# Values turned by VectorE and rewritten through memory instead of transposed on TensorE, and four steps of the last phase put in another order

## The chip, the cores and the metric

One core of one Trainium2 chip runs the kernel. The metric is the device time of one execution in microseconds (us); the median of the runs is compared. Engines in the profile: PE is TensorE's matmul, PEld its weight load, DVE is VectorE, ACT is ScalarE, POOL is GpSimd, SP is SyncE (here it issues all transfers).

## The reference: what is computed

A decoder layer on 1024 tokens of width 1024, in float32. Three groups of attention heads (head size 64) read one input projection of the normalised rows; a memory group of 4 heads reads 256 memory tokens.

```
h = rmsnorm(x, norm_w);  proj = h @ w_in
sb_q, sb_k, sb_v, fx_q, fx_k, fx_v, f_logit, m_q, gate = split(proj)
sb_out = stick_breaking_attention(sb_q, sb_k, sb_v)      # 8 heads
fx_out = forgetting_attention(fx_q, fx_k, fx_v, cumsum(log_sigmoid(f_logit + b)))   # 8 heads
m_out  = memory_attention(m_q, rmsnorm(mem) @ w_mem_kv)  # 4 heads
y = per_head_rmsnorm(concat(sb_out, fx_out, m_out)) * out_norm_w * silu(gate)
out = rmsnorm(x + y @ w_out, final_norm_w)
```

## The kernel before

**Stages.** After a start of about 60 us (rows squared, scaled and turned into `hT`, memory keys and values), the kernel runs ten phases, numbered 0 to 9: two of the memory heads, then `fx` and `sb` in turn, four pairs of heads each (phases 2, 4, 6, 8 are forgetting attention, 3, 5, 7, 9 stick-breaking). A phase is 16 ticks, one for each block of 128 queries of a head and half; the first and third group of four ticks have the long rows (640 to 1024 keys), the others the short ones (128 to 512). Ticks are counted through: phase 9 (`LAST`) begins at tick 144 (`X0`), and eight more ticks follow tick 159.

**A tick.** Every engine has its own list, written out tick by tick, and the order in it is fixed. TensorE does the scores of the tick (`scores`, L1023 and L1024), some steps of the projection (`project`, L867 to L869; in the last phase the output projection, L912), then the value products of the tick before (`values`, L1056 and L1057), the transposes of finished probability rows (`transposes`, L1037), the small transposes (`small`) and more projection. ScalarE makes the upper part of each transposed tile (`upper_part`, L1266), VectorE the lower one (`lower_part`, L1876), both needed by the value products of the next tick. Each float32 matrix is used as an upper and a lower part whose sum is the value.

**The values.** The projection leaves a head pair's values as 128 channels by 512 tokens in a bank, twice for a phase (`c` 0 and 1). VectorE copies them to `v_raw` (L1710; in `negL` or in a row of `work`). TensorE transposes the four blocks of 128 (`small`, piece "VT", L984) into `SMALL_BANK`, ScalarE copies the upper part to the heads' region (`values_hi`, L1223), VectorE subtracts for the lower one (`finish_small`, L1774). This stands in phase p-1 for phase p, for p from 2 to 9. The memory values ("MT") go the same way, and totals ("NT") too. Other pieces of the list `SMALL` don't touch TensorE: N1 (squares of the outputs summed per head) and N3 (the outputs' scale and the gate).

**Weights.** Tiles of 512 KB come through one buffer `w_raw`: `load_tile` (L606, L610) waits until ScalarE (L1165) and GpSimd (L1534) have split the tile before. SyncE does its list in order: behind `load_tile` stand the copies of the keys (L615, L616), `load_negL` (L625), the store of the scales (L649) and their spread fetch (L667).

**The last phase.** From tick 142 on SyncE fetches the split output weights (`fetch_w_out`, L713, 20 transfers of 512 KB), then blocks of the finished outputs (`load_y`, L722), split by ScalarE (`y_hi`, L1358) and VectorE (`y_lo`, L1890), and rows of x (`load_x`, L735) that are added to the partial outputs (L1730) and stored (L739). The gate of the last phase lies in `w_raw`, which is also a place for rows of x: it is stored in `silu_dram` (L814), and `load_x(1)` waits for that. At the end the last phase's own outputs are added: `end_outputs` (L1077), four calls with n from 0 to 3 and two later; call n from 2 on waits for the sum n-2 (`end_sum`, L1950), which for n below 4 waits for the partial rows (`load_part`, L744). The first call waits for the last scales (N3 at tick 165: L1811, L1816, then `y_end_hi` L1383 and `y_end_lo` L1895).

## Time and profile before

| | |
|---|---|
| median of 3 runs | 793.46 us (793.13 to 793.98) |
| profiled execution, its own time | 793.03 us |
| its span, first to last instruction | 791.1 us, so 1.9 us lie around it |
| PE busy | 776.6 us, 98% |
| DVE, ACT, POOL busy | 605.0, 445.7, 257.7 us (76%, 56%, 33%) |
| granted TensorE clock, mean | 0.998 of full speed |
| DMA queue of SyncE | 37648 packets, 92.50 MB, 36.1% of 16 engines |

The busy time of PE is that of matmuls that overlap in the pipeline, and their ends are modelled; a start and the next start tell more. Starts of one line in the timeline are the engine's own.

### The profile page before, as it was taken

The numbers are of one execution on the slowest core, as the hardware profiler recorded it, in microseconds if no ns is written. First come the engines' busy times: TensorE is split into PE (matmuls) and PEld (weight loads), VectorE is DVE, ScalarE is ACT, GpSimd is POOL, SyncE is SP. The second block draws the span as 40 slices with busy tenths as digits, with TensorE's granted clock in tenths as the row PEclk, the third lists the DMA queues.
The fourth block names the chain that finished last, engine by engine and source line by source line (L and its number), as shares of the span: only waits on it lengthen the run. The fifth ranks groups of instructions, "written<-read, shape, count | busy, mean of one in ns | idle before, by whom it ended". The sixth has DMA issues, their size and how long they took to land.

```text
span 791.1 us, 11916 instructions
## 1 busy us (share of the span) xinstructions
PE 776.6 (98%) x4030; PEld 653.2 (83%) x4030; DVE 605.0 (76%) x1206; ACT 445.7 (56%) x920; POOL 257.7 (33%) x440
## 2 busy tenths in 40 slices
PE   8999999999999999999999999999999999999997
PEld 8878887888888888888888888888888887878775
DVE  6877687776789777768977777898767688685676
ACT  7767765556646555665745667465555574542232
POOL 1112733242156326223823521383234124210000
PEclk9999999999999999999999999999999999999999
DMA  9413824124113412521261142106213398233523
GB/s 355 134 63 141 278 98 148 54 69 106 67 54 98 144 40 69 134 67 54 65 175 41 68 125 77 54 27 178 76 55 81 110 386 300 82 107 107 187 96 143
DMA packets 37708, 93.25 MB, mean 118 GB/s; under 512 B 5000, under 2 KB 13192, under 8 KB 36624
## 3 DMA queue, kind: packets, MB, share of 16 engines
q1 hardware_dynamic: 37648, 92.50, 36.1%
q8 instruction: 32, 0.52, 0.3%
q14 instruction: 28, 0.23, 0.1%
HBM read 61.91 MB, written 21.66 MB: 106 GB/s over the span
## 4 chain that ended last, share of the span: by engine, by line
PE 85%; DVE 7%; DMA 2%; ACT 2%; issue 2%; SPq 0%; POOL 0%; ACTq 0%; DVEq 0%; POOLq 0%
PE banks L867 16%; PE banks L869 15%; PE banks L868 15%; PE banks L1037 8%; PE banks L912 8%; PE banks L1057 5%; PE banks L1024 4%; PE banks L1056 4%; PE banks L1023 4%; PE banks L1108 1%; DMA hT<-wo_dram 1%; PE banks L984 1%; DMA work<-part_dram 1%; PE banks L1077 1%; DVE pT L1876 1%
## 5 line engine op out<-in xcount | busy, mean ns | idle before, releaser
L867 PE MATMUL banks<-hT,w_parts 128*128 128x512 f32 x576 | 237.6, 412 | 0.3 <-DVE sb_heads L1735 0.2
L869 PE MATMUL banks<-hT,w_parts 128*128 128x512 f32 x576 | 225.8, 392 | 0.0
L868 PE MATMUL banks<-hT,w_parts 128*128 128x512 f32 x576 | 225.4, 391 | 0.0
L1266 ACT ACTIVATE pT<-banks 128x512 fp32r<-128x512 f32 x208 | 92.4, 497 | 126.7 <-PE banks L1037 126.4
L1876 DVE TENSOR_TENSOR pT<-banks,pT 128x512 fp32r<-128x512 f32 x208 | 108.4, 563 | 66.6 <-ACT pT L1266 65.3
L869 PEld LDWEIGHTS banks<-hT,w_parts 128*128 128x128 f32 x576 | 108.1, 188 | 24.5
L867 PEld LDWEIGHTS banks<-hT,w_parts 128*128 128x128 f32 x576 | 108.5, 188 | 15.8 <-DVE sb_heads L1735 1.0
L868 PEld LDWEIGHTS banks<-hT,w_parts 128*128 128x128 f32 x576 | 109.0, 189 | 13.6
L1534 POOL TENSOR_TENSOR w_parts<-w_raw,w_parts 128x1024 fp32r<-128x1024 f32 x34 | 81.4, 2395 | 91.9 <-ACT w_parts L1165 91.9
L1541 POOL TENSOR_SCALAR_AFFINE_SELECT work<-work 128x128 f32<-128x128 f32 x64 | 30.4, 475 | 192.7 <-ACT work L1243 192.7
L1836 DVE TENSOR_TENSOR_SCAN work<-work 128x639 f32<-128x639 f32 (+3 forms) x64 | 90.7, 1418 | 0.7 <-POOL work L1541 0.6
L1242 ACT ACTIVATE work<-banks 128x512 f32<-128x512 f32 (+2 forms) x96 | 47.4, 494 | 71.5 <-PE banks L1024 60.3
L1037 PE MATMUL banks<-ident,work 128*128 128x128 f32 x640 | 87.1, 273 | 0.0
L1037 PEld LDWEIGHTS banks<-ident,work 128*128 128x128 f32 x640 | 74.8, 140 | 10.0
L912 PE MATMUL banks<-hT,fx_heads 128*128 128x512 f32 x288 | 73.6, 395 | 1.3 <-DMA hT<-wo_dram 1.3
L912 PEld LDWEIGHTS banks<-hT,fx_heads 128*128 128x128 f32 x288 | 52.7, 188 | 11.9 <-DMA hT<-wo_dram 1.7
L1259 ACT ACTIVATE work<-work,npeak 128x640 f32<-128x640 f32 (+3 forms) x64 | 49.7, 777 | 18.9 <-DVE npeak L1865 18.8
L1842 DVE TENSOR_TENSOR work<-work 128x639 f32<-128x639 f32 (+3 forms) x64 | 52.0, 813 | 6.6
L1856 DVE CUSTOM_DVE_ANT_0 work<-banks,negL 128x512 f32<-128x512 f32 (+3 forms) x56 | 32.1, 574 | 21.7 <-PE banks L1024 20.5
L1243 ACT ACTIVATE work<-banks 128x512 f32<-128x512 f32 (+2 forms) x96 | 47.7, 497 | 0.0
L1552 POOL TENSOR_SCALAR_AFFINE_SELECT diag<-negL 128x128 f32<-128x128 f32 x64 | 21.1, 333 | 73.1 <-DVE npeak L1865 73.0
L1023 PE MATMUL banks<-sb_heads 128*128 128x256 f32 (+2 forms) x128 | 41.5, 324 | 1.1 <-issue 1.0
(258 smaller groups left out, 1355.9 us busy)
## 6 DMA issues: line engine op xcount, KB each, us to landing
w_raw<-in_w_tiles SPq DMA_DIRECT2D x36, 512.0 KB, 3.9
hT<-wo_dram SPq DMA_DIRECT2D x14, 512.0 KB, 8.4
fx_heads<-fx_heads SPq DMA_DIRECT2D x8, 512.0 KB, 7.8
negL<-negL_dram SPq DMA_DIRECT2D x8, 512.0 KB, 6.1
yT_dram<-silu SPq DMA_DIRECT2D x8, 512.0 KB, 4.1
sb_heads<-sb_heads SPq DMA_DIRECT2D x8, 512.0 KB, 6.7
negL<-yT_dram SPq DMA_DIRECT2D x8, 512.0 KB, 4.9
work<-in_x SPq DMA_DIRECT2D x6, 512.0 KB, 6.7
```

Source lines behind the costliest of these rows:

```text
L867: pe.matmul(o, w[0][:, k, :], hT[:, 0, k, tok], start=(k == 0), stop=False)
L868: pe.matmul(o, w[0][:, k, :], hT[:, 1, k, tok], start=False, stop=False)
L869: mm = pe.matmul(o, w[1][:, k, :], hT[:, 0, k, tok], start=False, stop=(k == KT - 1))
L912: mm = pe.matmul(banks[:, bank_of(q + c - p.c), :], yt, wo_part(j, r)[:, c, :], start=(fresh and j == order[0] and (l, r) == (0, 0)), stop ...
L1023: pe.matmul(o, q, k[:, 0, c0:c1], start=True, stop=False)
L1037: mm = pe.transpose(banks[:, T_BANK + n % 2, j * P:(j + 1) * P], p_row(u + j)[:, t.s * P:(t.s + 1) * P], ident[:, :])
L1259: act.activation(p_row(u), p_row(u), ACT.Exp, bias=top, accum_out=total).then_inc(fx_p, 1)
L1266: act.activation(pT[:, n % 3, 0, cols], banks[:, T_BANK + n % 2, cols], ACT.Copy).then_inc(t_hi, 1)
L1534: pool.tensor_tensor(w_part(n, 1), by_tiles(w_raw_of(n)), w_part(n, 0).bitcast(F32), ALU.subtract).then_inc(w_lo, 1)
L1836: dve.tensor_tensor_scan(left, left, left, 1.0, ALU.mult, ALU.bypass).then_inc(scanned, 1)
L1842: dve.tensor_tensor(b[:, 0:w - 1], b[:, 0:w - 1], f[:, 1:w], ALU.mult).then_inc(sb_p, 1)
L1876: dve.tensor_tensor(pT[:, n % 3, 1, cols], banks[:, T_BANK + n % 2, cols], pT[:, n % 3, 0, cols].bitcast(F32), ALU.subtract).then_inc(t_lo, 1)
```

## The change

The values are no longer transposed by TensorE. VectorE writes `v_raw` with a transpose of 32x32 blocks, SyncE stores it in a buffer in memory with four transfers per piece that put the blocks at their transposed places (runs of 32 numbers, 128 bytes), and fetches it in rows of 512 bytes to the place of the lower part. ScalarE copies it to the upper part, VectorE subtracts in place. Two waits that told when `v_raw` was free now ask for the store. Ticks: the fetch is at tick 7 of the phase (or later), the two splits at ticks 13 and 15 of it (for phase 9 at ticks 141 and 143; for phase 3 at 45 and 47; for phase 2 at 21 and 25). The plan of the projection steps stays as it is. In the last phase the store of the gate moves behind the fetches of the output weights, `y_hi` and `y_lo` move behind `upper_part` and `lower_part` (and behind the tick's small pieces), and the last N3 moves ahead of `output`.

```diff
-READY_BEFORE = firsts(1 if p.what in ("VT", "MT", "NT") else 0 for p in SMALL)
+def values_ticks():
+    out = []
+    for of in range(2, N_PH):
+        for c in range(2):
+            done = READ_TICK[piece_of("V", c, of)] - 1
+            fetch = max(done + 2, UNITS * (of - 1) + 7) if of > 2 else done + 8
+            out.append((of, c, fetch, max(fetch + 3, UNITS * (of - 1) + 13 + 2 * c) if of > 2 else fetch + 3))
+    return out
@@ sync
+                if p.what == "V":
+                    store_values(q)
                 if closes_tile(p) and p.what == "K":
                     copy_keys(p.of, q)
+            def store_values(q):
+                p = PIECE[q]
+                sp.wait_ge(piece_done, q + 1)
+                rows = v_dram[p.of, p.c, :, :].rearrange("(j k) (i d) -> i k j d", k=Q4, d=Q4)
+                for i in range(P // Q4):
+                    sp.dma_start(rows[i], v_raw(p.of, p.c)[i * Q4:(i + 1) * Q4, :].rearrange("k (j d) -> k j d", d=Q4)).then_inc(v_out[p.c], 16)
+            def fetch_values(of, c):
+                sp.wait_ge(v_out[c], 64 * (of - 1))
+                if of > 2:
+                    sp.wait_ge(pv_done, STEP0[4 * (of - 1)])
+                else:
+                    for j in (1, 2):
+                        sp.wait_ge(wo_out[j], 32)
+                sp.dma_start(v_in_rows(of, c).bitcast(F32).rearrange("p b x c -> p b (x c)"),
+                             v_dram[of, c, :, :].rearrange("(b p) w -> p b w", p=P)).then_inc(v_in[c], 16)
+                if c == 1 and PHASES[of][0] == "fx":
+                    load_negL(PHASES[of][1], 1)
-                if p.what == "VT" and p.c == 1 and PHASES[p.of][0] == "fx":
-                    sp.wait_ge(small_done, n + 1)
-                    load_negL(PHASES[p.of][1], 1)
@@ sync, last phase
-            sp.wait_ge(piece_done, piece_of("G", 1, LAST) + 1)
-            sp.dma_start(silu_dram[:, :], gate_of(LAST)).then_inc(silu_out, 16)
             sp.wait_ge(piece_ready, piece_of("G", 1, LAST - 1) + 1)
             for j in range(6, NB):
                 fetch_w_out(j)
             for j in range(NB, NT_OUT):
                 fetch_w_out(j)
+            sp.wait_ge(piece_done, piece_of("G", 1, LAST) + 1)
+            sp.dma_start(silu_dram[:, :], gate_of(LAST)).then_inc(silu_out, 16)
             load_x(1)
@@ tensor
-                if p.what == "VT":
-                    pe.wait_ge(piece_done, piece_of("V", p.c, p.of) + 1)
-                    for b in range(4):
-                        mm = pe.transpose(o[:, b * P:(b + 1) * P], v_raw(p.of, p.c)[:, b * P:(b + 1) * P], ident[:, :])
-                    pe.wait_ge(small_done, small_of("VT", 1, x0.ph) + 1)
+                    pe.wait_ge(v_done, 2 * (x0.ph - 1))
@@ scalar
+            def values_hi(of, c):
+                act.wait_ge(v_in[c], 16 * (of - 1))
+                act.activation(v_of(region_of(of))[:, 4 * c:4 * c + 4, 0::3, :], v_in_rows(of, c).bitcast(F32), ACT.Copy).then_inc(v_hi, 1)
-                    act.wait_ge(small_ready, READY_BEFORE[small_of("VT", 1, t.ph)] + 1)
+                    for c in range(2):
+                        act.wait_ge(v_out[c], 64 * (t.ph - 1))
-                for n in Y_AT[i]:
-                    y_hi(n)
                 if 1 <= i <= N_UNITS and UNIT[i - 1].kind != "sb" and not softmax_ends:
...
+                for of, c, _, at in VALUES:
+                    if i == at:
+                        values_hi(of, c)
+                for n in Y_AT[i]:
+                    y_hi(n)
@@ vector
-                    dve.tensor_copy(v_raw(p.of, p.c), src).then_inc(piece_done, 1)
+                    dve.transpose(v_raw(p.of, p.c), src).then_inc(piece_done, 1)
+            def values_lo(of, c):
+                dve.wait_ge(v_hi, 2 * (of - 2) + c + 1)
+                v = v_of(region_of(of))[:, 4 * c:4 * c + 4, :, :]
+                dve.tensor_tensor(v[:, :, 1:3, :], v[:, :, 1:3, :].bitcast(F32), v[:, :, 0::3, :].bitcast(F32), ALU.subtract).then_inc(v_done, 1)
-                for n in Y_AT[i]:
-                    y_lo(n)
+                ended = [n for n in SMALL_AT[i] if (SMALL[n].what, SMALL[n].of) == ("N3", LAST)]
+                for n in ended:
+                    finish_small(n)
                 if i in OUT_AT:
                     output(OUT_AT[i])
...
                 for n in T_AT[i]:
                     lower_part(n)
+                for of, c, _, at in VALUES:
+                    if i == at:
+                        values_lo(of, c)
...
+                for n in Y_AT[i]:
+                    y_lo(n)
```

## Rows read from the trace of the kernel before

**Rows 1.** The page: the engines' busy time over the span.
```profile
PE 776.6 (98%) x4030; PEld 653.2 (83%) x4030; DVE 605.0 (76%) x1206; ACT 445.7 (56%) x920; POOL 257.7 (33%) x440
```
**Rows 2.** The largest wait of PE from 60 us on: total us, times, longest.
```profile
PE banks L1056 <- DVE pT L1876: 1.4, 2, 1.1
```
**Rows 3.** Timeline of PE around one value transposition: start us, length us.
```profile
118.19 0.39 PE L869 MATMUL banks<-hT,w_parts 128*128 128x512 f32 x1
118.42 0.60 PE L984 MATMUL banks<-ident,negL 128*128 128x128 f32 x4
118.78 0.48 PE L867 MATMUL banks<-hT,w_parts 128*128 128x512 f32 x1
119.09 0.40 PE L868 MATMUL banks<-hT,w_parts 128*128 128x512 f32 x1
```
**Rows 4.** Groups by line, whole span: count, busy us, mean ns, idle before.
```profile
L984 PE MATMUL banks<-ident,negL 128*128 128x128 f32 x32 | 4.8, 273 | 0.0
L1710 DVE COPY work<-banks 128x512 f32<-128x512 f32 x8 | 5.5, 684 | 0.0
L1790 DVE STREAM_TRANSPOSE o_tmp<-banks 128x512 f32<-128x512 f32 x20 | 14.1, 705 | 1.7 <-ACT banks L1287 1.7
L1383 ACT ACTIVATE sb_heads<-silu 128x512 fp32r<-128x512 f32 x2 | 1.3, 632 | 3.2 <-DVE silu L1816 3.2
```
**Rows 5.** The largest wait of ACT, 129 to 640 us: total us, times, longest.
```profile
ACT pT L1266 <- PE banks L1037: 102.7, 61, 3.8
```
**Rows 6.** Transfers: packets and the scales' store alone (314 to 317.5 us), then a median.
```profile
q1 hardware_dynamic: 144, 0.02, 3.1%
...
r_dram<-r_rows SPq DMA_DIRECT2D x1, 16.0 KB, 1.4
...
negL<-yT_dram SPq DMA_DIRECT2D x8, 512.0 KB, 4.9
```
**Rows 7.** Timeline of SyncE in phase 3: issues of two weight tiles, start us.
```profile
238.65 0.33 SPq L610 DMA_DIRECT2D w_raw<-in_w_tiles  x1
250.81 0.33 SPq L610 DMA_DIRECT2D w_raw<-in_w_tiles  x1
```
**Rows 8.** Timeline at the start of the last phase, ACT and then PE.
```profile
635.60 0.48 ACT L1243 ACTIVATE work<-banks 128x384 f32<-128x384 f32 x1
636.14 0.51 PE L1023 MATMUL banks<-sb_heads 128*128 128x512 f32 x1
```
**Rows 9.** Last phase: two stalls of PE; one window (its last two numbers: DMA share, GB/s).
```profile
658.99 0.98 PE L912 MATMUL banks<-hT,fx_heads 128*128 128x512 f32 x3 [1.31 <-DMA hT<-wo_dram]
704.22 0.47 PE L1056 MATMUL banks<-pT,sb_heads 128*128 128x512 f32 x1 [1.11 <-DVE pT L1876]
...
652.30:653.60 1.30, 1.30 (x7) 1.08 (x6) 1.20 (x2) 0.00 (x0) 0.00 (x0) 1.00 1.04 403
```
**Rows 10.** Timeline of DVE and ACT, ticks 157 and 163 to 165.
```profile
701.41 1.23 DVE L1890 TENSOR_TENSOR fx_heads<-negL,fx_heads 128x1024 fp32r<-128x1024 f32 x1 [0.87 <-ACT fx_heads L1358]
733.46 0.63 ACT L1297 ACTIVATE work<-head 128x512 f32<-128x512 f32 x1 [4.75 <-DVE head L1683]
736.94 0.71 DVE L1811 STREAM_TRANSPOSE banks<-work 128x512 f32<-128x512 f32 x1
738.47 0.63 ACT L1383 ACTIVATE sb_heads<-silu 128x512 fp32r<-128x512 f32 x1 [2.96 <-DVE silu L1816]
```
**Rows 11.** The chain that ended last, its steps from 734 to 752 us.
```profile
733.99 1.05 ACT fx_heads L1358
735.07 1.24 DVE fx_heads L1890
736.32 0.37 SPq L722
...
743.37 1.24 DVE work L1950
...
752.19 3.02 PE banks L1077 x12
```

More of the change, by code:

```diff
@@ L290, in small_pieces @@
             out.append(Small("N3", c, ph - 1, UNITS * ph + N3_AT + N3_LATER.get(ph - 1, 0)))
-    taken = [p.tick for p in out]
-    for q, p in enumerate(PIECE):
-        if p.what == "V":
-            tick = max(READ_TICK[q] + 1, UNITS * (p.of - 1) + (9 + 2 * p.c if p.of == 2 else 6))
-            while tick in taken:
-                tick += 1
-            taken.append(tick)
-            out.append(Small("VT", p.c, p.of, tick))
     for c in (1, 0):
@@ L307 @@
 SMALL_AT = [[n for n, p in enumerate(SMALL) if p.tick == i] for i in range(N_TICKS)]
-READY_BEFORE = firsts(1 if p.what in ("VT", "MT", "NT") else 0 for p in SMALL)
+READY_BEFORE = firsts(1 if p.what in ("MT", "NT") else 0 for p in SMALL)
 NT_BEFORE = firsts(1 if p.what == "NT" else 0 for p in SMALL)
-VT_BEFORE = firsts(1 if p.what in ("VT", "MT") else 0 for p in SMALL)
+MT_BEFORE = firsts(1 if p.what == "MT" else 0 for p in SMALL)
+def values_ticks():
[6 more added lines that the diff above has]
+    return out
+VALUES = values_ticks()
 def next_phase(i, at, later={}):
@@ L444, in v_raw, with v_in_rows @@
             return place[:, c * CW:(c + 1) * CW]
+        def v_in_rows(of, c):
+            return v_of(region_of(of))[:, 4 * c:4 * c + 4, 1:3, :]
         def gate_of(ph):
@@ L794, in _ @@
                     piece_end(q)
+                for of, c, fetch, _ in VALUES:
+                    if i == fetch:
+                        fetch_values(of, c)
                 for n in SMALL_AT[i]:
@@ L977, in small @@
                 p = SMALL[n]
-                if n and p.what in ("VT", "MT", "NT"):
+                if n and p.what in ("MT", "NT"):
                     pe.wait_ge(small_done, n)
                 o = banks[:, SMALL_BANK, :]
-                if p.what == "VT":
-                    pe.wait_ge(piece_done, piece_of("V", p.c, p.of) + 1)
-                    for b in range(4):
-                        mm = pe.transpose(o[:, b * P:(b + 1) * P], v_raw(p.of, p.c)[:, b * P:(b + 1) * P], ident[:, :])
-                elif p.what == "MT":
+                if p.what == "MT":
                     pe.wait_ge(piece_done, piece_of("memV", p.c, None) + 1)
@@ L1207, in split_next, with mem_values_hi @@
                     split_hi(w_follows(PIECE[q].tile))
-            def values_hi(n):
+            def mem_values_hi(n):
                 p = SMALL[n]
                 act.wait_ge(small_ready, READY_BEFORE[n] + 1)
-                if p.what == "MT":
-                    for b in range(MB):
-                        ins = act.activation(mem_v[:, b, p.c, 0::3, :],
-                                             banks[:, SMALL_BANK, b * P:(b + 1) * P].rearrange("p (h c) -> p h c", h=2), ACT.Copy)
-                    ins.then_inc(vt_hi, 1)
-                    return
-                if p.of > 2:
-                    act.wait_ge(pv_done, STEP0[4 * (p.of - 1)])
-                elif p.c == 0:
-                    for j in (1, 2):
-                        act.wait_ge(wo_out[j], 32)
-                act.activation(v_of(region_of(p.of))[:, 4 * p.c:4 * p.c + 4, 0::3, :],
-                               banks[:, SMALL_BANK, :].rearrange("p (b h c) -> p b h c", b=4, h=2), ACT.Copy).then_inc(vt_hi, 1)
+                for b in range(MB):
+                    ins = act.activation(mem_v[:, b, p.c, 0::3, :],
+                                         banks[:, SMALL_BANK, b * P:(b + 1) * P].rearrange("p (h c) -> p h c", h=2), ACT.Copy)
+                ins.then_inc(mt_hi, 1)
+            def values_hi(of, c):
+                act.wait_ge(v_in[c], 16 * (of - 1))
+                act.activation(v_of(region_of(of))[:, 4 * c:4 * c + 4, 0::3, :], v_in_rows(of, c).bitcast(F32), ACT.Copy).then_inc(v_hi, 1)
             def sigmoids(u):
@@ L1442, in _ @@
             for n in range(len(MEM_VALUES_AT)):
-                values_hi(n)
+                mem_values_hi(n)
             evacuate(7)
@@ L1490, in _ @@
                 for n in SMALL_AT[i]:
-                    if SMALL[n].what in ("VT", "MT"):
-                        values_hi(n)
+                    if SMALL[n].what == "MT":
+                        mem_values_hi(n)
                     if SMALL[n].what == "N1" and SMALL[n].of == LAST:
@@ L2082, in _ @@
                     lower_part(n)
+                for of, c, _, at in VALUES:
+                    if i == at:
+                        values_lo(of, c)
                 for n in SMALL_AT[i]:
-                    if n not in early:
+                    if n not in early + ended:
                         finish_small(n)
```

11 lines of the change are left out of this document (4 added, 7 removed).

## The prediction

> **What bounds the kernel now.** I read the page first: PE is busy 98% of the span, DVE 76%, ACT 56% [rows 1]. A busy PE can hide stalls here, since matmuls overlap in the pipeline and their ends are modelled, so I read PE's waits next. From 60 us on the largest of them is 1.4 us in all [rows 2]; the reader is to see that over 700 us nothing else keeps PE waiting for longer. The counter-view is the waits of ACT: in 500 us of the middle it waited 102.7 us for PE's transposes, 61 times, 1.7 us each on average [rows 5]. The engines behind PE wait for it, not it for them. So PE's own instructions set the pace, and one that disappears from PE's list is worth its distance from start to start. In the last phase it is different: there PE has two stalls of over 1 us [rows 9], and the chain that ended last leaves PE for ACT, DVE, SyncE and a transfer [rows 11].
>
> **Term 1: the transposes on PE.** Phases 2 to 9 have two pieces of values each, so 16 groups of four transposes go, 64 instructions, in two groups of 32 of which one is shown [rows 4]. What is one group worth? From the start of the matmul ahead (118.19) to the start of the second behind (119.09) it is 0.90 us [rows 3]. Without the four, two starts of 512 columns would lie there, 0.23 us each by the first pair of the same rows (118.19 to 118.42), 0.46 in all. That leaves 0.44 us. In most ticks other transposes (L1037) stand just ahead, and a first matmul behind transposes is longer by some 0.08 us (118.78 to 119.09 is 0.31), which may stay; so 0.36 to 0.44 is the bound from both sides, 5.8 to 7.0 us for 16. I take 7.0, since the 0.36 is only the distance to the first matmul and what stays is paid by the groups ahead anyway. The mean of 273 ns per transpose [rows 4] would give 17.5 us; it holds the modelled drain and I don't take it. The Trainium skill, page "Perfetto Trace Analysis", section "Identifying the Most-Contended Engine", says that TensorE's matmul busy time is a bad measure, because matmuls are pipelined; by busy durations the sum would be 10.5 us better than by starts. The trace sides with that rule: the row of four says 0.60 us of length, while the next matmul starts after 0.36.
>
> **Term 2: what VectorE and ScalarE do instead.** The copy of 684 ns becomes a 32x32 transpose of the same shape, 705 ns in the row nearest to it, 16 times 0.02 us. The upper part is now read from SBUF, 632 ns in the nearest row [rows 4]; the subtraction keeps its size. Under the cover of PE all this costs nothing. It moves: for the phases with long rows the splits leave ticks 7 and 8 (two of the dense ones) for ticks 13 and 15, whose rows are short. Cover gone, it would be 32 pieces of 0.65 us, 21 us, but only where ACT has less than the 1.7 us it waits on average. One place has no cover: the upper part for phase 9 at tick 143. Behind it on ScalarE stand the y block, the exponentials, a table load and the first sigmoids of phase 9, and PE's second scores wait for a bank that these read: the read started at 635.60, lasted 0.48, and PE started at 636.14 [rows 8]. That is 0.06 us behind it, so no slack. One ACT step more, 0.63 less the overlap of neighbours, is **+0.5 us** on PE (bounds 0 and 0.63). I take it for this phase alone, since for the others no y block stands between.
>
> **Term 3: the transfers.** Each piece is stored by four transfers of 512 packets of 128 bytes, 2048 in all, and fetched in 512 packets of 512 bytes. 16 such stores are 32768 packets, nearly as many as the kernel has. No row shows such a store, so I bound it. Below: the scales' store, 128 packets of 128 bytes, landed in 1.4 us, and 144 packets took 3.1% of 16 engines in 3.5 us, 12 ns of an engine each [rows 6]. With that, 2048 packets over 16 engines add 1.5 us, some 3 us to landing. Above: if the whole 1.4 us were per packet, 16 times 1.4 are 22 us. The nearest row in count is the fetch of y, 1024 packets of 512 bytes in 4.9 us; twice that is 10 us. I take 3 to 7 us. Who waits for it? SyncE itself, which asks for the store ahead of the fetch. In phase 3 the store follows the weight tile of 238.65, and the next thing that SyncE does late is the tile of 250.81, for which it waits anyhow [rows 7]. Between them lie 12 us, so a store of 7 us and a fetch of 4 us are hidden, and the splits come only at ticks 13 and 15. `load_negL`, which stood in the crowd behind 250.81, now goes out ahead of it; a small relief, no gain on PE. I take **0**.
>
> **Term 4: the gate's store behind the weights.** PE waits at 658.99 for the fetched output weights; to the idle 1.31 us come 0.16 that the modelled end hides (0.39 of length against 0.23 between starts, rows 3), 1.47 in all. The DMA engines are full there; the gate's 512 KB take 1.3 us of them (403 GB/s, share 1.04) [rows 9]. Taken out of the queue ahead, every later weight lands 1.3 us earlier, and PE comes 0.5 later by term 2: the stall goes, **-1.5 us** (bounds -1.0 and -1.5). What is late next: `load_x(1)` and the y block 2 behind it go out only once it has landed behind all of these weights. ScalarE may wait for the block, but it does so behind the upper parts of its tick, and PE needs the block two ticks on.
>
> **Term 5: blocks behind transposed parts.** At 704.22 PE waits for the lower part of tick 157: 1.11 idle, 1.27 with the hidden 0.16 [rows 9]. Ahead of that part DVE did the y block, 1.23 us, and sat idle 0.87 for it [rows 10]. Both move behind it, 2.1 us against a stall of 1.27: it goes, **-1.3 us**.
>
> **Term 6: the same move at the end, and the last scales first.** Here the rule turns. The chain that ended last runs: y block 6 on ACT (733.99) and DVE (735.07, done 736.31), the issue of y block 7 by SyncE (736.32), behind it final norm weights and the partial rows, the first sum on DVE (743.37), the last head sums, the second sum, and PE's fourth end call at 752.19 [rows 11]. In the new order tick 165 has the scales first. They can start when the spread is there, 733.46 + 0.63 = 734.09. From the start of their turn to the end of ScalarE's copy it was 736.94 to 739.10, 2.16 us [rows 10], so 736.25 now. Only then does ScalarE begin y block 6, 1.05 us, and DVE its lower part, 1.24: done at 738.5 instead of 736.3. All that SyncE issues behind it, y block 7 and the partial rows, is late by 2.2 us, and so are both sums and PE's fourth call: **+2.2 us**. What the scales first bring, the end of PE's wait of 0.84 idle us ahead of its first call, doesn't count, since the fourth call waits anyhow. Bounds: +2.2 where the chain holds, and -1.0 where the partial rows have slack that I don't see.
>
> **Sum.** -7.0 + 0.5 + 0 - 1.5 - 1.3 + 2.2 = -7.1 us. Against the profiled execution's own time, 793.03, that is 785.9; the median of the runs is 0.4 higher, so **786.4 us**. Its own range, with the bounds of the terms, is 785.9 to 788.2 (1.2 more by term 1, 0.1 by term 2, 0.5 by term 4; 0.5 less by term 2).
>
> **Rivals.**
> - *The end doesn't give it back* (12%): the sums are early enough, and the scales' wait goes. Then 3.2 us less, 783.2. For it: nothing in the rows, except that 7 us pass from the issue at 736.32 to the sum at 743.37, in a crowd of transfers that could thin out. Against it: the first three steps of rows 11 follow each other within 0.03 us.
> - *ACT and DVE take over* (12%): the value transposes stood between a step's transposes and its products and gave ACT and DVE 0.4 us more to make the parts. Where that was the last slack, PE now waits. For it: DVE is at 76% [rows 1], and that is a mean over phases of which some must be denser. Against it: 1.7 us of average wait. If half the groups pay, the first term is -3.5: 789.9.
> - *Small packets hold SyncE, and it ends slower* (4%): store and fetch together over 12 us delay the next weight tile and the keys' copies in phases 3, 5 and 7. At the upper bound of 22 us and a fetch of 4, SyncE is 14 us late in each; if all of it reaches PE, 42 in all, 828. It is slower than before from 2.4 us of lateness a phase, a store of about 10.4 us. The Trainium skill, page "VectorE: DVE Perf Modes", section "The three transpose paths", warns that a plain DMA copy that transposes by strides is 19 times slower than the hardware's own way. The 12 ns per packet of 128 bytes speak against it here.
> - *Nothing comes of it* (4%): what PE saves is lost at a phase's start where Q and keys are waited for: 793.
>
> **Numbers.** Forecast 68%. The range that leaves out less than 2 in 10 reaches from the first rival to the second: 783.2 to 789.9. A measurement of this kernel tells 0.2%, 1.6 us, from nothing. Faster: forecast and the first two rivals, 92%; same 4%; slower 4%.
>
> **What would show it.** L984 gone, and PE's starts 0.23 apart where it stood; the small-packet count up by 32768, with each of the four store transfers landing in 3 to 7 us; no wait of PE for wo_dram and none at tick 158; the start of phase 9 with about 0.5 us more of a wait for ACT; and y block 7 issued 2 us later counted from the last transposes, with the fourth end call waiting some 3 to 4 us for a sum. It would be wrong if L1266 or L1876 now release PE in the middle, if a store of values takes above 10 us to land, or if the partial rows come early.

## The result, and the profile after

The changed kernel takes **805.05 us** (median of 4 runs, 803.12 to 805.27) beside 793.72 (793.13 to 795.39) for the kernel before on the same chip: ratio 1.0137, interval 1.0125 to 1.015. It is slower by 11.3 us where 7.1 us of gain were forecast, and lies outside the range of the prediction. The profiled execution took 803.12 us, the fastest of the four, and its span is 801.4 (before: 791.1).

The page of the changed kernel, its engines and packets, and then the mean granted clock of the core (before: 0.998):

```profile
PE 775.8 (97%) x3966; PEld 650.3 (81%) x3966; DVE 611.2 (76%) x1206; ACT 446.5 (56%) x920; POOL 260.9 (33%) x440
...
PEclk9999998999999999999999999999999999999999
...
DMA packets 79949, 101.65 MB, mean 127 GB/s; under 512 B 39048, under 2 KB 55432, under 8 KB 78864
```
```profile
core 0: 801.4 us, clock 0.990
```

PE has 64 instructions less than in [rows 1], as meant, and is busy for 0.8 us less in a span that is 10.3 us longer. The packets under 512 bytes went from 5000 to 39048. One slice of the clock fell from 9 to 8: the seventh, 120 to 140 us.

The waits of the changed kernel (total us, times, longest):

```profile
PE banks L1053 <- ACT work L1282: 8.9, 2, 6.5
PE banks L1107 <- DVE work L1979: 4.5, 1, 4.5
...
ACT fx_heads L1249 <- DMA fx_heads<-v_dram: 9.8, 2, 7.2
```

Before, the largest wait of PE from 60 us on was 1.4 us [rows 2]. Now PE waits 8.9 us, in two pieces, for an exponential of ScalarE, and the last row says for what ScalarE waits: the upper part of the values (L1249) that a transfer brings back from DRAM. The other new wait, 4.5 us, is the fourth end call of PE.

Where along the kernel the time goes shows best when the start of the same unit of work is read in both traces, a unit's first scores matmul. The table is worked out so, start after minus start before; the last entry is the difference of the spans:

```
tick    22    24     28     30     36     48     64     66     70     74
us   +0.25 +4.00 +11.82 +12.39 +12.01 +11.15 +10.78 +11.47 +11.47 +10.61
tick    96     98    102    106   119   122   134   138   144   145   149   150   158   159   end
us   +9.93 +10.51 +10.51  +9.65 +9.68 +8.81 +8.96 +8.10 +8.10 +8.62 +8.63 +7.48 +7.48 +6.05 +10.3
```

So 12.1 us are lost between ticks 22 and 30, the second half of phase 1, in which the values for phase 2 are made ready. Then the curve falls by 0.41 to 0.45 wherever four transposes are gone, as term 1 had it, rises by 0.69 where phase 4 starts, by 0.58 where phase 6 does and by 0.52 at phase 9 (tick 145), falls by 1.1 at the gate's store (tick 150) and by 1.4 at tick 159, and rises by 4.25 at the end. (Rises of 0.3 and less in between, 0.9 us together, I did not follow.)

**The values for phase 2.** ScalarE of the changed kernel, timeline, at the two upper parts for phase 2 (start us, length us, in brackets the idle time ahead of it and what ended it), and PE where it waits for them:

```profile
109.99 0.63 ACT L1249 ACTIVATE fx_heads<-fx_heads 128x512 fp32r<-128x512 f32 x1 [2.64 <-DMA fx_heads<-v_dram]
...
127.09 0.63 ACT L1249 ACTIVATE fx_heads<-fx_heads 128x512 fp32r<-128x512 f32 x1 [7.20 <-DMA fx_heads<-v_dram]
127.63 0.46 ACT L1282 ACTIVATE work<-banks,npeak 128x256 f32<-128x256 f32 x1
```
```profile
111.65 0.38 PE L1053 MATMUL banks<-sb_heads 128*128 128x256 f32 x1 [2.46 <-ACT work L1282]
...
128.23 0.58 PE L1053 MATMUL banks<-sb_heads 128*128 128x256 f32 x1 [6.48 <-ACT work L1282]
...
129.25 0.63 PE L902 MATMUL banks<-hT,w_parts 128*128 128x512 f32 x1
129.68 0.63 PE L903 MATMUL banks<-hT,w_parts 128*128 128x512 f32 x1
130.10 0.63 PE L901 MATMUL banks<-hT,w_parts 128*128 128x512 f32 x1
...
132.89 0.39 PE L901 MATMUL banks<-hT,w_parts 128*128 128x512 f32 x1
133.12 0.40 PE L902 MATMUL banks<-hT,w_parts 128*128 128x512 f32 x1
```

The exponential that PE waits for at 128.23 (L1282, 127.63) isn't late by itself; it stands behind the upper part on ScalarE, which is blocked for 7.20 us by a fetch. And the wait is not the whole loss. Behind it PE's matmuls of 512 columns start 0.43 us apart (129.25, 129.68, 130.10) and not 0.23 as at the end of the fence: that is the lower of the clock's two levels, 1.2 GHz. Summed over the two places, the starts are 12.9 us further apart than in undisturbed rows: 8.94 of it are the two idle times, 0.3 what the modelled ends hide of them, and 3.6 matmuls at or near the lower clock. The two groups of transposes that are gone here give 0.9 back.

Why does the fetch come so late? SyncE of the changed kernel, timeline, and the instruction of GpSimd that its weight tile waits for:

```profile
104.22 1.13 SPq L665 DMA_DIRECT2D fx_heads<-v_dram  x1
122.90 0.34 SPq L621 DMA_DIRECT2D w_raw<-in_w_tiles  x1
123.34 0.37 SPq L665 DMA_DIRECT2D fx_heads<-v_dram  x1
```
```profile
120.45 2.38 POOL L1563 TENSOR_TENSOR w_parts<-w_raw,w_parts 128x1024 fp32r<-128x1024 f32 x1
```

The second fetch (123.34) could have gone out much earlier (fetch_early, below, issues it at 104), but SyncE stood from 105.35 to 122.90 at the weight tile ahead of it in its list, which needs the room that GpSimd's split frees at 122.83. The fetch landed at 127.07 and took only 3.7 us. In the kernel before, the same tile was issued at 119.47 and PE did not wait in that stretch. This chain is that of the second piece. The first piece's fetch did not stand behind the tile: it was issued at 104.22 and took 5.7 us to land, in a stretch in which the DMA engines were busy with the split output weights, a tile and the next piece's stores (95 to 112 us: the queue's packets take 83.9% of 16 engines). By the table above (ticks 22 to 30) the first piece cost some 4 us and the second some 8.

**The transfers.** The page of the changed kernel, its DMA issues (KB each, median us from issue to landing):

```profile
v_dram<-negL SPq DMA_DIRECT2D x32, 64.0 KB, 3.2
...
fx_heads<-v_dram SPq DMA_DIRECT2D x8, 256.0 KB, 3.1
v_dram<-work SPq DMA_DIRECT2D x32, 64.0 KB, 2.6
```

A store of 512 packets of 128 bytes lands in 2.6 to 3.2 us in the median, the 64 of them in 1.7 to 5.6. Term 3 had taken 3 to 7.

**The end.** The chain that ended last, of the changed kernel (start us, us), with the steps that answer to [rows 11], and a timeline of GpSimd and DVE there:

```profile
742.27 1.06 ACT fx_heads L1384
743.35 2.04 DVE fx_heads L1919
745.41 0.37 SPq L753
...
746.50 5.87 DMA work<-part_dram
...
752.47 1.24 DVE work L1979
...
760.00 1.23 DVE work L1979
761.27 4.32 PE banks L1107 x12
```
```profile
742.57 1.73 POOL L1594 TENSOR_TENSOR silu<-silu,yT 128x512 f32<-128x512 f32 x1 [14.07 <-DVE yT L1914]
...
743.35 2.03 DVE L1919 TENSOR_TENSOR fx_heads<-negL,fx_heads 128x1024 fp32r<-128x1024 f32 x1 [0.20 <-ACT fx_heads L1384]
```

From the issue of y block 7 to the first sum it takes 7.06 us (before 7.05), from there to the second 7.53 (before 7.56): the chain moved as a whole. Its head moved by 9.09 us (736.32 to 745.41), PE by 6.05, so the end is late by 3.04. Of these 2.2 are the ones of term 6; the other 0.8 is the lower part of block 6, which took 2.03 us and not 1.23 as in [rows 10]. Then come the twelve matmuls, 4.32 us in place of 3.02, the first six of them again at the lower clock.

### The profile page after: what moved, and what is told of

Same layout as the page of the kernel before. It is cut to its first block, busy times and chain, and to the rows that moved or that the text cites. A ratio compares the mean times of both kernels' runs of the same rounds, so it can differ in the third digit from the quotient of the medians.

```text
span 801.4 us, 11859 instructions
## 1 busy us (share of the span) xinstructions
PE 775.8 (97%) x3966; PEld 650.3 (81%) x3966; DVE 611.2 (76%) x1206; ACT 446.5 (56%) x920; POOL 260.9 (33%) x440
## 4 chain that ended last, share of the span: by engine, by line
PE 83%; DVE 6%; DMA 3%; ACT 3%; issue 2%; POOL 1%; SPq 1%; ACTq 0%; DVEq 0%; POOLq 0%
PE banks L901 15%; PE banks L903 15%; PE banks L902 15%; PE banks L946 9%; PE banks L1067 8%; PE banks L1053 4%; PE banks L1087 4%; PE banks L1054 4%; PE banks L1086 4%; DMA fx_heads<-v_dram 1%; PE banks L1138 1%; PE banks L1107 1%; DMA hT<-wo_dram 1%; DMA work<-part_dram 1%; POOL w_parts L1563 1%
## 5 line engine op out<-in xcount | busy, mean ns | idle before, releaser
L1292 ACT ACTIVATE pT<-banks 128x512 fp32r<-128x512 f32 x208 | 92.4, 497 | 124.5 <-PE banks L1067 124.2
L1905 DVE TENSOR_TENSOR pT<-banks,pT 128x512 fp32r<-128x512 f32 x208 | 108.3, 562 | 59.0 <-ACT pT L1292 57.8
L1570 POOL TENSOR_SCALAR_AFFINE_SELECT work<-work 128x128 f32<-128x128 f32 x64 | 32.6, 509 | 184.8 <-ACT work L1269 184.8
L1067 PEld LDWEIGHTS banks<-ident,work 128*128 128x128 f32 x640 | 74.8, 140 | 10.1
```

The source lines that it names most:

```text
L1067: mm = pe.transpose(banks[:, T_BANK + n % 2, j * P:(j + 1) * P], p_row(u + j)[:, t.s * P:(t.s + 1) * P], ident[:, :])
L1292: act.activation(pT[:, n % 3, 0, cols], banks[:, T_BANK + n % 2, cols], ACT.Copy).then_inc(t_hi, 1)
L1905: dve.tensor_tensor(pT[:, n % 3, 1, cols], banks[:, T_BANK + n % 2, cols], pT[:, n % 3, 0, cols].bitcast(F32), ALU.subtract).then_inc(t_lo, 1)
```

## The experiments

Each median stands beside that of the kernel before, measured on the same chip in the same session: 793.51 us for vals_only, order_only, split_late and big_packets; 793.97 for y6_early, scales_late, splits_13_14 and best_a; 793.87 for fetch_early, rows_first, gate_early and best_b. Line numbers shift by at most 2 between the versions of the changed kernel; order_only has those of the kernel before.

### vals_only: the values' path alone
The changed kernel with the whole last phase in the order of before (the gate's store, the y blocks, the last scales).
```
             fetch_w_out(0)
+            sp.wait_ge(piece_done, piece_of("G", 1, LAST) + 1)
+            sp.dma_start(silu_dram[:, :], gate_of(LAST)).then_inc(silu_out, 16)
...
                     sigmoids(i)
+                for n in Y_AT[i]:
+                    y_hi(n)
...
                     turn_scales(ph)
-                ended = [n for n in SMALL_AT[i] if (SMALL[n].what, SMALL[n].of) == ("N3", LAST)]
-                for n in ended:
-                    finish_small(n)
+                for n in Y_AT[i]:
+                    y_lo(n)
```


> The values' new path alone, the last phase in its old order. Theory A (the values for phase 2 are fetched too late, ScalarE waits for them in ticks 21 and 25 and PE behind it; it costs 12 us; the end of the last phase costs about 2 us more): 802.3 us, stalls of PE of 2.5 and 6.5 us near 112 and 128 us, and the sum at the end on time, with no wait of PE above 1.1 us there. Theory B (the 32768 small packets slow all engines' accesses and transfers everywhere): also about 802 to 805, but spread over phases 2 to 8.

Measured: 801.3 us (799.63 to 802.29), ratio 1.0098 [1.008, 1.0115], span 798.7. PE has both waits for phase 2's values, 2.39 and 6.34 us, and not the one of 4.5 at the end. The values' path alone loses 7.8 of the 11.3 us; what the last phase loses shows in the next run.

### order_only: the last phase alone
The kernel before with the four steps in the last phase and its values left as they were: the edit of vals_only the other way round, made to the kernel before.
```
             fetch_w_out(0)
-            sp.wait_ge(piece_done, piece_of("G", 1, LAST) + 1)
-            sp.dma_start(silu_dram[:, :], gate_of(LAST)).then_inc(silu_out, 16)
...
                     turn_scales(ph)
-                for n in Y_AT[i]:
-                    y_lo(n)
+                ended = [n for n in SMALL_AT[i] if (SMALL[n].what, SMALL[n].of) == ("N3", LAST)]
+                for n in ended:
+                    finish_small(n)
```

> The kernel before with the four steps of the last phase reordered, no new path for the values. Theory A: the stalls at 659 and 704 us go (-2.7), the partial rows land later and PE's fourth end call waits 4.5 us and then runs at the lower clock for a while (+4.3): 795.3, slower than before by 1.6. Rival (the reorder is a gain, the loss at the end comes from the values' transfers): 791.0, no long wait at the end.

Measured: 796.14 us (794.93 to 797.56), ratio 1.0034 [1.0023, 1.0045], span 793.4. Unit by unit against the kernel before, it is 1.1 us earlier behind the gate's store and another 1.4 at tick 159, as terms 4 and 5 had it, and then loses 4.6. PE, timeline, the fourth end call:

```profile
753.00 2.44 PE L1077 MATMUL banks<-w_parts,fx_heads 128*128 128x512 f32 x6 [4.51 <-DVE work L1950]
755.23 2.38 PE L1077 MATMUL banks<-hT,sb_heads 128*128 128x512 f32 x6
```

Six matmuls take 2.23 us from start to start of the two rows, where 1.49 are the rule (in y6_early the same two starts are 746.13 and 747.62). The last phase's steps by themselves lose 2.6 us; with the values' 7.8 that is 10.4 of the 11.3.

### split_late: phase 2's splits 8 and 6 ticks later
```
-            out.append((of, c, fetch, max(fetch + 3, UNITS * (of - 1) + 13 + 2 * c) if of > 2 else fetch + 3))
+            out.append((of, c, fetch, max(fetch + 3, UNITS * (of - 1) + 13 + 2 * c)))
```
For phase 2 the splits now stand at ticks 29 and 31 and not at 21 and 25. The fetches stay where they are, behind the weight tile.

> The changed kernel, but the two splits of phase 2's values stand at ticks 29 and 31 instead of 21 and 25; the fetches and all packets stay. Theory A: both stalls near 112 and 128 us go and the clock stays up: 805.05 - 12.3 = 792.7. Theory B (packets): at most 2 us better, 803.

Measured: 791.97 us (791.04 to 793.87), ratio 0.9982 [0.9972, 0.9991]. ScalarE, timeline, the same two upper parts:

```profile
124.17 0.63 ACT L1249 ACTIVATE fx_heads<-fx_heads 128x512 fp32r<-128x512 f32 x1
128.91 0.61 ACT L1249 ACTIVATE fx_heads<-fx_heads 128x512 fp32r<-128x512 f32 x1
```

No idle time ahead of either, and no wait of PE for L1282 above 0.02 us. One condition taken out turns 1.4% slower into 0.2% faster. The same stores and fetches are all there; what cost the time was asking for their result too early. The new ticks have a smaller price of their own. VectorE's subtraction of the second piece now falls beside GpSimd's split of a tile (129.09, 2.37 us), and PE waits behind it where phase 2 starts, DVE and then PE:

```profile
129.56 2.45 DVE L1846 TENSOR_TENSOR fx_heads<-fx_heads 128x512 fp32r<-128x512 f32 x1 [0.21 <-ACT fx_heads L1249]
...
134.16 0.50 PE L1053 MATMUL banks<-fx_heads 128*128 128x512 f32 x1 [0.77 <-DVE peak L1885]
```

### big_packets: the same bytes in few packets
```
-                for i in range(P // Q4):
-                    sp.dma_start(rows[i], v_raw(p.of, p.c)[i * Q4:(i + 1) * Q4, :].rearrange("k (j d) -> k j d", d=Q4)).then_inc(v_out[p.c], 16)
+                sp.dma_start(v_dram[p.of, p.c, :, :].rearrange("(p r) w -> p (r w)", p=P), v_raw(p.of, p.c)).then_inc(v_out[p.c], 16)
```
One store of 128 rows of 2 KB in place of four of 512 packets each. The edit leaves out the blocks' move to their transposed places, so this kernel computes with mixed-up values and serves for its time alone. It changes two things at once: the packets' size, and what SyncE has to issue, one store for a piece and not four.

> The changed kernel, but each piece of values is stored in one transfer of 128 rows of 2 KB instead of four transfers of 512 packets of 128 bytes; the blocks' new places are left out of the computation, so the values are mixed up. Ticks, waits and all else stay. Theory A: the second and larger stall (6.6 us) stays, since SyncE stands behind a weight tile's wait and not behind packets; the first (2.6 us) may shrink, as SyncE issues faster in phase 1: 801 to 805. Theory B: 793 or less.

Measured: 801.97 us (800.52 to 803.1), ratio 1.0105 [1.009, 1.012], span 801.3 (the changed kernel: 801.4). Packets and ScalarE of this run:

```profile
DMA packets 48461, 101.65 MB, mean 127 GB/s; under 512 B 5512, under 2 KB 21896, under 8 KB 47376
```
```profile
107.75 0.63 ACT L1247 ACTIVATE fx_heads<-fx_heads 128x512 fp32r<-128x512 f32 x1 [0.57 <-DMA fx_heads<-v_dram]
124.83 0.63 ACT L1247 ACTIVATE fx_heads<-fx_heads 128x512 fp32r<-128x512 f32 x1 [7.84 <-DMA fx_heads<-v_dram]
```

The small packets are gone, and the wait for the second fetch is 7.84 us, longer than in the changed kernel. The first fetch's wait does fall, from 2.64 to 0.57: it is issued at 100.48 and not at 104.22. So 2.3 us of this loss (10.1 us at tick 30 and not 12.4) hang on the four stores, by their packets or by their issues, which this run doesn't tell apart; the large wait doesn't. That the two spans are equal is chance: behind its fourth end call this execution gives 2.1 us back, where its twelve matmuls take 5.29 us and not 4.17 because the lower clock lasts longer. Each beside its own kernel before, the medians stand 2.9 us apart.

### fetch_early: the second fetch ahead of the weight tile
```
-            fetch = max(done + 2, UNITS * (of - 1) + 7) if of > 2 else done + 8
-            out.append((of, c, fetch, max(fetch + 3, UNITS * (of - 1) + 13 + 2 * c) if of > 2 else fetch + 3))
+            fetch = max(done + 2, UNITS * (of - 1) + 7) if of > 2 else done + (8 if c == 0 else 7)
+            out.append((of, c, fetch, max(fetch + 3, UNITS * (of - 1) + 13 + 2 * c) if of > 2 else done + 11))
```
The splits of phase 2 stay at 21 and 25; only the fetch of the second piece goes out one tick earlier in SyncE's list, which is ahead of the tile.

> The changed kernel with one thing moved: the fetch of phase 2's second piece stands at tick 21 of SyncE's list, ahead of the weight tile of tick 22, not behind it. Splits stay at ticks 21 and 25. Theory A (the 6.6 us stall is SyncE's wait for GpSimd's split of the tile ahead, not the landing): that stall goes with the lower clock behind it, 7.7 us; the first stall of 2.6 stays: 805.05 - 7.7 = 797.3. Rival (the landing itself is slow in that stretch): 803 or more.

Measured: 798.3 us (797.77 to 798.38), ratio 1.0053 [1.0038, 1.0068]. SyncE issues both fetches together, and ScalarE doesn't wait for the second:

```profile
103.59 1.79 SPq L665 DMA_DIRECT2D fx_heads<-v_dram  x2
...
123.73 0.34 SPq L621 DMA_DIRECT2D w_raw<-in_w_tiles  x1
```
```profile
110.81 0.63 ACT L1249 ACTIVATE fx_heads<-fx_heads 128x512 fp32r<-128x512 f32 x1 [3.34 <-DMA fx_heads<-v_dram]
...
120.48 0.63 ACT L1249 ACTIVATE fx_heads<-fx_heads 128x512 fp32r<-128x512 f32 x1
```

The splits stand where they stood, the packets are the same, and the 7.2 us are gone: it was the order in SyncE's list. What stays is the first fetch, 3.34 us on ScalarE and 3.15 on PE, and six matmuls of 512 columns at the lower clock behind it. And PE waits 1.30 us at 125.36 for an exponential. The rows show its cause, the subtraction of the second piece on VectorE, which takes 2.83 us in place of 0.69 beside GpSimd's split of a tile and holds the row maxima (L1899) behind it:

```profile
121.35 2.83 DVE L1846 TENSOR_TENSOR fx_heads<-fx_heads 128x512 fp32r<-128x512 f32 x1
...
121.25 2.39 POOL L1563 TENSOR_TENSOR w_parts<-w_raw,w_parts 128x1024 fp32r<-128x1024 f32 x1
```

### y6_early: the block of tick 165 back in its old place
split_late, and for tick 165 alone the y block stands ahead of the parts again.
```
+                for n in Y_AT[i] if i == END_N3_TICK else []:
+                    y_hi(n)
...
+                for n in Y_AT[i] if i == END_N3_TICK else []:
+                    y_lo(n)
```


> split_late, with the one y block of tick 165 (block 6) ahead of the scales and the output again, on ScalarE and VectorE; the other six blocks stay behind the transposed parts. Theory A (the late partial rows hold the second sum, PE's fourth end call waits 4.7 us and runs at the lower clock for some 2.5 us after it): both losses go, 791.97 - 6.3 = 785.7. Rival (the wait comes from the store of the gate behind the weights, which shifts the rows of x and with them the partial rows): no change, 792.

Measured: 787.1 us (786.69 to 787.49), ratio 0.991 [0.9895, 0.9924], mean clock 1.0. The fourth end call waits 1.01 us, not 4.51, and its matmuls run at the higher clock. Some 5 us come from one y block's place (4.9 between the medians, 5.3 with each beside its own kernel before).

### rows_first: only SyncE's order at the end
split_late, and y block 7 goes out behind the final norm's weights and the partial rows.
```
             for n in range(6):
-                load_y(n + 2)
+                if n < 5:
+                    load_y(n + 2)
...
                 load_part(n)
+            load_y(7)
```


> split_late, with y block 7's load on SyncE behind the final norm weights and the four partial rows instead of ahead of them. Orders of ScalarE and VectorE stay as changed, so y block 6 is as late as in the change. Theory A (PE's 4.7 us wait at the end runs over SyncE's list: block 6, then the load of block 7, which waits for it, then the partial rows): the wait and the lower clock go, 791.97 - 6 = 786. Rival (the wait comes over ScalarE's and VectorE's own later work): 791 to 792.

Measured: 786.0 us (785.75 to 786.67), ratio 0.9901 [0.9886, 0.9916]. SyncE and PE, timelines:

```profile
719.63 2.76 SPq L775 DMA_DIRECT2D work<-part_dram  x3
733.62 0.37 SPq L753 DMA_DIRECT2D negL<-yT_dram  x1
```
```profile
744.97 1.67 PE L1109 MATMUL banks<-w_parts,fx_heads 128*128 128x512 f32 x6
```

Block 6 is as late here as in split_late (its lower part takes 2.03 us in both), but the partial rows don't stand behind it, and PE has no idle time of note at the fourth call. The head of the chain in [rows 11] was late only through SyncE's list.

### scales_late: without the last scales first
split_late with the last scales turned where they were.
```
-                ended = [n for n in SMALL_AT[i] if (SMALL[n].what, SMALL[n].of) == ("N3", LAST)]
-                for n in ended:
-                    finish_small(n)
...
-                    if n not in early + ended:
+                    if n not in early:
```

> split_late, with the last scales behind the output again; the y blocks stay late. Theory A: the y block's place does it, the scales' own move is a small gain: the block ends another 0.7 us later, so 792.7. Rival (the scales ahead of everything at tick 165 are what holds the block): the wait shrinks by 2 us or more, 789.

Measured: 792.57 us (791.8 to 793.63), ratio 0.9984 [0.9974, 0.9993]; the wait of 4.51 us at the fourth call is there. The scales' place is worth 0.6 us at most: the delay comes from the block's place, not from theirs. On ScalarE the block still stands behind the copy of the scales here (L1409 at 730.85, block 6 at 731.38); it starts later than in split_late, and its lower part takes 1.22 us and not 2.03.

### gate_early: the gate's store ahead of the weights again
y6_early with the store of `silu_dram` in front of the fetches of the output weights.
```
             fetch_w_out(0)
+            sp.wait_ge(piece_done, piece_of("G", 1, LAST) + 1)
+            sp.dma_start(silu_dram[:, :], gate_of(LAST)).then_inc(silu_out, 16)
```

> y6_early with the gate's store ahead of the weights' fetches again, as in the kernel before. Theory A: PE waits for the weights 1.2 us longer: 787.1 + 1.2 = 788.3. Rival (the store's place is worth nothing): 787.1.

Measured: 789.07 us (788.56 to 789.59), ratio 0.9941 [0.9924, 0.9957], 2.0 us above y6_early in its medians. PE, timeline:

```profile
656.05 0.96 PE L946 MATMUL banks<-hT,fx_heads 128*128 128x512 f32 x3 [1.27 <-DMA hT<-wo_dram]
```

The stall of [rows 9] is back, 1.27 us there and none above 0.15 in y6_early: term 4 is shown, and rather above its 1.5.

### splits_13_14: the second split one tick earlier
Since PE waits where phases 4 and 6 start, split_late with
```
-            out.append((of, c, fetch, max(fetch + 3, UNITS * (of - 1) + 13 + 2 * c)))
+            out.append((of, c, fetch, max(fetch + 3, UNITS * (of - 1) + 13 + c)))
```

> split_late, with the second split at tick 14 of each phase instead of tick 15. Theory A: the waits of PE at the first ticks of phases 4, 6 and 9 (0.6, 0.6 and 0.8 us) come from that split standing just ahead of the phase's first reads; 0.6 + 0.6 + 0.5 go: 790.2. Rival (they come from the transfers or from less cover on PE): 792.

Measured: 791.03 us (790.06 to 791.87), ratio 0.996 [0.9946, 0.9974]. Half right. The waits at the starts of phases 4 and 6 (0.40 and 0.41 us in split_late) are gone, phase 9's falls from 0.60 to 0.10 and phase 2's from 0.77 to 0.41, but where phases 5 and 7 start PE now sits 1.12 us where it had sat 0.52:

```profile
336.86 0.41 PE L1053 MATMUL banks<-sb_heads 128*128 128x384 f32 x1 [1.12 <-issue]
```

The split at tick 14 or 15 is thus what PE meets at a phase's start, and either tick hits another kind of phase. For phase 2 the second subtraction is now done before GpSimd begins its split at 128.76, and takes 0.68 us where it took 2.45 in split_late; tick 33 starts 0.64 us earlier:

```profile
125.82 0.68 DVE L1846 TENSOR_TENSOR fx_heads<-fx_heads 128x512 fp32r<-128x512 f32 x1
```

### best_a and best_b: the two put together
best_a is y6_early with `13 + c`; best_b has the later tick in phases 5 and 7 only:
```
+            out.append((of, c, fetch, max(fetch + 3, UNITS * (of - 1) + 13 + (2 if of in (5, 7) else 1) * c)))
```

> split_late with both of the changes above, block 6 early and the second split at tick 14: 791.97 - 6.3 - 1.7 = 784.0 by theory A, 792 by the rivals. Against the kernel before it would be 9.5 us, 7.0 of them the transposes on PE.

> y6_early, with the second split at tick 14 for all phases but 5 and 7, where it stays at tick 15 (at tick 14 PE waited 0.6 us more at the start of these two). Theory A: best_a less 2 x 0.6: 786.14 - 1.2 = 784.9. Rival: same as best_a, 786.1.

Measured: 786.14 us (785.93 to 786.84), ratio 0.9899 [0.9884, 0.9914], and 786.35 us (785.91 to 786.51), ratio 0.9903 [0.9889, 0.9918]. The second doesn't beat the first, though its waits in phases 5 and 7 are those of y6_early. At tick 112 it is 0.9 us ahead of best_a by the compared starts; then PE waits 0.55 us for output weights (none of note in best_a) and 1.48 at the fourth end call (1.16 in best_a), and that call starts at 745.31 in both. What was won in the middle was waited away in the last phase; what sets that moment was not tried. rows_first, best_a and best_b can't be told from each other: 786.0 to 786.4, 1% below the kernel before.

## Why the prediction was wrong, step by step

**The step that failed is term 3, "I take 0".** It asked who waits for the stores and fetches, and answered from phase 3: "a store of 7 us and a fetch of 4 us are hidden, and the splits come only at ticks 13 and 15". In phases 3 to 9 ScalarE indeed never waits for a fetch. It doesn't hold for phase 2, whose ticks the new `values_ticks` sets by another branch (`else done + 8`, `else fetch + 3`): fetched at ticks 18 and 22 and split three ticks later. Ahead of the second fetch, in the same tick, stands the tile for which SyncE waits for GpSimd. The chain, all of it in rows above: GpSimd's split, weight tile, fetch, upper part on ScalarE, exponential, PE; that is some 8 us of the 12.1 net. The other 4 are the first fetch, split three ticks after it was asked for while it took 5.7 us to land. vals_only puts it into the values' path, split_late takes it away by moving the reader, fetch_early takes away its larger half by moving the fetch alone, and big_packets leaves that half there with 33,500 small packets less. To see it beforehand, term 3 had to be worked out at phase 2's ticks as well, and set beside the row of before in which the same tile goes out only at 119.47.

The rival of the other side, "Small packets hold SyncE, and it ends slower", had the place right (SyncE) and the cause wrong. It made its price from the time of a store, whose median was 2.6 to 3.2 us; SyncE was held by the tile's wait, 17.5 us, which big_packets has as well. On the page of the Trainium skill weighed there, "VectorE: DVE Perf Modes", section "The three transpose paths": the page gives its factor of 19 for a large innermost destination stride, a condition that the prediction left out. Here VectorE had turned the 32x32 blocks first and the store's innermost run is 128 bytes; no run here has a copy with such a stride.

**Not counted at all: the clock.** No term had a price for what PE does after a long wait. It is 3.6 us behind the two waits for phase 2's values and 1.25 at the end (the excess of the fourth call's first six matmuls over six starts of 0.228 us, 1.36 us, less the 0.11 that they had before), 4.9 us of the 17.4 between the sum of -7.1 and the spans' +10.3.

**Term 1 (-7.0) right.** 0.41 to 0.45 us per group in the trace, 0.43 in the mean, where its bounds were 0.36 and 0.44; 16 of them are 6.9 us. PE where such a group stood, now with only the other transposes ahead of the weights' matmuls (the changed kernel, timeline):

```profile
247.96 0.93 PE L1067 MATMUL banks<-ident,work 128*128 128x128 f32 x7
248.65 0.47 PE L901 MATMUL banks<-hT,w_parts 128*128 128x512 f32 x1
248.96 0.39 PE L902 MATMUL banks<-hT,w_parts 128*128 128x512 f32 x1
```

The first distance behind them is 0.31 us, as in [rows 3]: what stays was paid by the groups ahead. By durations it would have been 17.5 us; the starts were the right measure.

**Term 2 (+0.5) right in its place, too small in its reach.** At tick 145 the shift rises by 0.52, and PE waits there for a sigmoid:

```profile
644.76 0.50 PE L1053 MATMUL banks<-sb_heads 128*128 128x512 f32 x1 [0.61 <-ACT work L1269]
```

"I take it for this phase alone" was wrong: phases 4 and 6 start 0.69 and 0.58 later too, and splits_13_14 shows by removing these waits that it is the second split. The durations of the transposes (702 to 707 ns) and the upper parts (632) were right. "The subtraction keeps its size" was not: the old one read a bank, the new one has both inputs in SBUF, and where it met GpSimd's split it took up to 2.83 us (fetch_early).

**Term 4 (-1.5) right:** -1.15 in the changed kernel, -1.1 in order_only, and 2.0 us in the medians of gate_early. In the changed kernel 0.16 us of the wait is left, as the weights land with PE close behind.

**Term 5 (-1.3) right:** -1.4 in both. No experiment moved that block alone.

**Term 6 (+2.2) right in its mechanism, half the size:** +4.25 in the changed kernel. 2.2 of the chain's delay as worked out; 0.8 because DVE's add took 2.03 us; 1.25 by the clock. Here the prediction had said 3 to 4 us for the fourth call's wait, and it was 4.5.

The first two rivals didn't come: the end did give it back, until y6_early or rows_first stopped it, and neither L1292 nor L1905 has PE wait in the middle for longer than before. With the phase 2 splits late and the end in order the kernel takes 786.0 us, where the prediction said 786.4. That is no proof of the sum: terms 2 and 6 have other sizes in it.

## What to carry to other kernels

When a new transfer goes through a queue that issues in order, find for every phase, the first and the special ones above all, what that queue waits for ahead of the transfer, and not only how long the transfer takes: here 3.7 us of transfer came 17.5 us late. Put the reader a few ticks later where it can wait, and look at what it meets there: split_late won 13 us so, and paid some 0.6 us where phase 2 starts. An instruction waiting on ScalarE holds all that stands behind it, exponentials that PE needs included. Price a long wait of TensorE above its length, since the matmuls behind it run slower for a while, and look in SyncE's order first when a chain at the end is late: the partial rows stood behind a block they had nothing to do with.

## What the runs showed of the hardware

**The clock after a wait.** After an idle time of 2.46 us on PE (and of 6.48, and of 4.52 at the end) the 512-column matmuls started 0.43 us apart and then 0.23 again: the lower of the two levels, 1.2 GHz in place of 2.4. It lasted for 2.8 to 4.4 us each time, and up to 5.8 behind the same wait at the end in other runs (scales_late). The shortest wait with this behind it is 2.39 us (vals_only), the longest without it 1.48 (best_b). y6_early and rows_first, with no long wait, have a mean clock of 1.000, the changed kernel 0.990.

**Small packets cost little.** 64 KB in 512 packets of 128 bytes landed in 2.6 to 3.2 us in the median. The Trainium skill, page "DMA: Bandwidth & Descriptors", section "Specifications", names 512 bytes as the least for full rate; no run here measures the rate. With 33,500 such packets and 48 issues less the kernel is 2.9 us faster by its medians, 2.3 us of it at the first fetch for phase 2, and its largest wait stays.

**One add, two durations.** The y block's lower part, 128x1024 with both inputs in SBUF, took 1.21 to 1.30 us in most places. At tick 165 of the changed kernel, order_only, split_late and rows_first it took 2.03 us, and in each GpSimd's product had begun 0.78 us ahead of it and lasted 1.73, so that 0.95 us of it lay beside the add; where only 0.33 us of a product lay beside it (the changed kernel at 728.17) it took 1.42. In y6_early, where the add comes ahead of the product, it is 1.23 again:

```profile
729.06 1.23 DVE L1921 TENSOR_TENSOR fx_heads<-negL,fx_heads 128x1024 fp32r<-128x1024 f32 x1 [1.04 <-ACT fx_heads L1384]
...
732.58 1.72 POOL L1596 TENSOR_TENSOR silu<-silu,yT 128x512 f32<-128x512 f32 x1 [16.16 <-DVE yT L1916]
```

The Trainium skill, page "SBUF — State Buffer", section "Who interferes with whom", says that a VectorE instruction with two SBUF inputs contends with a GpSimd instruction that reads SBUF, and that the second to issue is blocked. By that rule the add would end 1.23 us after GpSimd's end at 744.30, at 745.53; it ended at 745.38. The trace agrees to 0.15 us. So it does for the values' subtraction, 0.68 to 0.69 us alone. In fetch_early GpSimd's split ends at 123.64, by the rule the subtraction would end at 124.33, and it ended at 124.18; in split_late it would be 132.14, and it was 132.01. Where the overlap was taken away the length went with it: the subtraction in splits_13_14 and the add in y6_early, both moved ahead of GpSimd's instruction, and the add in scales_late, beside which no product ran (1.22).
